# Latent attention of a four-layer kernel: its products from split operands instead of plain float32

## The chip, the cores and the metric

The program runs on one core of one Trainium2 chip. Its time is device microseconds of that core, from one launch; every number for a kernel is the median of several runs. TensorE (PE) multiplies and writes PSUM; VectorE (DVE), ScalarE (ACT) and GpSimd (POOL) work beside it; SyncE (SP) issues most of the DMAs.

## The reference

The reference is a stack of four layers on 512 latent tokens (and, in the first layer, 256 context tokens) of width 1024. The change touches the first layer's mixer, a multi-head latent attention with 8 heads. Cut to what matters:

```python
h_all = concat([h_ctx, h_lat])                       # T = 256 + 512 tokens, width 1024
cq = rms_norm(h_all @ w_dq, g_q)                     # rank 384
q = (cq @ w_uq).reshape(T, 8, 128 + 64)              # per head: 128 plain, 64 rotary
ckv = h_all @ w_dkv
c_kv = rms_norm(ckv[..., :256], g_kv)                # rank 256
kv = (c_kv @ w_ukv).reshape(T, 8, 128 + 128)         # per head: keys and values
k_rope = ckv[..., 256:]                              # 64 rotary columns, shared by the heads
# the rotary parts of the latent tokens are rotated
s = (q_nope @ k_nope.T + q_rope @ k_rope.T) * 192 ** -0.5
o = softmax(s) @ v       # latent tokens see all 768 keys, context tokens the 256 of the context
y = o @ w_o
```

All numbers are float32. The output is the last layer's latent tokens.

## The kernel before, in words

Activations are held transposed (width on the 128 partitions, the T = 768 tokens along the free dimension), in an area of SBUF called `arena`, which is why a trace names most tiles of the attention `arena`. A stage is a row of `STAGES`: its name, its iterations, its weight groups and its PSUM units per iteration. Weight groups come through a ring of two slots, `wring`, loaded by SP; a slot's next load waits until the group after it has started on PE (`w_used`). PSUM is used as two accumulators `acc[0]` and `acc[1]` (two banks each), taken in turn by consecutive units: `claim` waits until a unit's accumulator is free, `finished` until its products are done, `emptied` until an engine has copied it out. Two more such pairs, `sc[0]` and `sc[1]`, hold the scores.

In most stages (those in `SPLIT`) the operands are split. ACT copies a float32 weight into `w_hi`, which is rounded to float32r (`high_weights`, L1710), DVE subtracts to get `w_lo` (`split_weights`, L2399), activations are split likewise, and `split_product` makes each product from three matmuls: high by high, high by low, low by high. The stage `mla_pair`, which is changed, isn't among them: before, it works in plain float32, for which the trace shows two PE instructions a product.

`mla_pair` runs four times, with two heads in each iteration. An iteration has two parts.

**The projections.** Group 0 (`w_uq`, 3 blocks of 384 columns) gives unit 0 and 1 (plain queries of the two heads) and unit 2 (rotary queries of both); group 1 (`w_ukv`, 2 blocks of 512) gives units 3 and 4 (keys) and 5 to 7 (values, 2 token tiles each). DVE copies each unit out (L2323, L2326). Then two small matmuls (units 8 and 9, L960) rotate the rotary queries, and DVE puts them together (L2328 to L2337). PE waits for that (`qrope_ready`) before the first score.

**The loop over 12 score tiles** (6 per head: two of 256 keys, four of 768). For tile n: `turn(n)` transposes the probabilities on PE (L979), `scores(n + 2)` makes the scores of the tile after the next (L968, L970), `weigh(n)` multiplies by the values (L988). DVE finds the maximum (L2348) and its negative (L2350), copies out the result of tile n - 2 (L2341), takes the reciprocal of the sum (L2354), and does `in_attention(n)`, work for a later stage that has nothing to do with the attention (L2238, L2240, L2268, L2270). ACT makes the exponentials and their sum (L1696), copies the transposed probabilities of tile n - 1 out of PSUM (`turned`, L1688), and scales tile n (L1701). `weigh(n)` waits for `turned(n)`, which stands on ACT behind the exponentials of tile n + 1.

After the fourth iteration ACT loads a table, takes a small activation, loads the old table again (L1569, L1749), and splits the first group of `mla_out`, the output projection, together with DVE; then the attention's output is split block by block (L1717, L2376), and PE starts on `mla_out`.

Of the kernel before, what the change touches and what calls it, by code (L numbers as in the profile page):

```python
# [34 lines left out]
for _name, _n in [  # L35
# [16 lines left out]
    ("mla_in", 1, 2, 6), ("mla_rope", 1, 0, 2), ("mla_pair", 4, 2, 34), ("mla_out", 1, 4, 8),  # L52
# [10 lines left out]
SPLIT = ("mla_out", "mlp0", "gla_head", "gla_out", "mlp1", "gdn_gate", "gdn_pair", "gdn_out", "ffn0_up", "ffn0_down", "ret_head", "ret_out",  # L63
         "ffn1_up", "ffn1_down")
# [84 lines left out]
def first_and_second_block(nc, A, out):  # L149
    ctx = ExitStack()  # L150
    with ctx:
# [24 lines left out]
        eps = sb("eps", [P, 2])  # L176
        sq = sb("sq", [P, 2, T])
# [19 lines left out]
        with ExitStack() as plain:  # L197
            first("hT_", [P, DB, T])
            first("before_x_hi", [P, 2 * DB * T])
            x_hi_seq = first("x_hi_seq", [P, DB, SEQ], F32R)  # L200
        attn_lo = overlay("attn_lo", DB * T + ATTN_AT, [P, MLA_H, T])
# [50 lines left out]
        cq = carve(3, T)  # L252
        ckv = carve(2, T)
# [141 lines left out]
        lat_ready, krope_ready = sem("lat_ready"), sem("krope_ready")  # L395
        qrope_ready, s_ready = sem("qrope_ready"), sem("s_ready")
# [74 lines left out]
        def hole_parts(k):  # L471

            return [(0, SEQ, x_hole(k), x_lo[:, k, CTX:T])]

# [279 lines left out]
        def _(pe):  # L754
# [177 lines left out]
            pe.wait_ge(lat_ready, 5)  # L932
            pe.wait_ge(krope_ready, 2)
            S = "mla_pair"
            with pe.Fori(0, MLA_H // 2) as it:
                wq = group(S, it, 0, 3, 384)
                pe.wait_ge(uq_in, it * 48 + 48)
                for j, m in ((0, 0), (1, NOPE)):
                    claim(pe, S, it, j)
                    linear(unit(S, j), wq, m, lambda k: cq[:, k, :], T, 3).then_inc(acc_ready, 1)  # L940
                claim(pe, S, it, 2)
                linear(unit(S, 2), wq, 2 * NOPE, lambda k: cq[:, k, :], T, 3).then_inc(acc_ready, 1)
                wkv = group(S, it, 1, 2, 512)
                for j, m in ((3, 0), (4, 256)):
                    claim(pe, S, it, j)
                    linear(unit(S, j), wkv, m, lambda k: ckv[:, k, :], T, 2).then_inc(acc_ready, 1)
                wv = wkv.rearrange("p k (h s n) -> p k h s n", h=2, s=2)
                for j in range(3):
                    claim(pe, S, it, 5 + j)
                    for i in range(2):  # L950
                        t = 2 * j + i
                        for k in range(2):
                            last = mm(unit(S, 5 + j)[:, i, 0:256], ckv[:, k, t * P:(t + 1) * P],
                                      wv[:, k, :, 1, :], k == 0, k == 1)
                    last.then_inc(acc_ready, 1)

                emptied(pe, S, it, 2)
                for j in range(2):
                    claim(pe, S, it, 8 + j)
                    pe.matmul(unit(S, 8 + j)[:, 0, 0:256], rot2, qraw[:, CTX + 256 * j:CTX + 256 * (j + 1)],  # L960
                              start=True, stop=True).then_inc(acc_ready, 1)
                pe.wait_ge(qrope_ready, it * 1 + 1)

                def scores(n):
                    e, t = n // QT, n % QT
                    spans = [(0, 0, CTX)] if t < 2 else [(h, h * HALF, HALF) for h in range(2)]
                    for h, k0, w in spans:
                        pe.matmul(sc[:, n % 2, h, 0:w], qn[:, e, t * P:(t + 1) * P], kn[:, e, k0:k0 + w],  # L968
                                  start=True, stop=False)
                        last = pe.matmul(sc[:, n % 2, h, 0:w], qr[:, t * P:(t + 1) * P], krope[:, e, k0:k0 + w],  # L970
                                         start=False, stop=True)
                    last.then_inc(s_ready, 1)

                def turn(n):
                    nk = 2 if n % QT < 2 else KT
                    pe.wait_ge(p_ready, it * 12 + n + 1)
                    claim(pe, S, it, 10 + 2 * n)
                    for k in range(nk):
                        last = pe.transpose(flat(unit(S, 10 + 2 * n))[:, k * P:(k + 1) * P],  # L979
                                            prob[:, n % 2, k * P:(k + 1) * P], ident)  # L980
                    last.then_inc(acc_ready, 1)

                def weigh(n):
                    e, nk = n // QT, 2 if n % QT < 2 else KT
                    claim(pe, S, it, 11 + 2 * n)
                    emptied(pe, S, it, 10 + 2 * n)
                    for k in range(nk):
                        last = pe.matmul(unit(S, 11 + 2 * n)[:, 0, 0:P], vtok[:, k, e * P:(e + 1) * P],  # L988
# [2090 lines left out]
```

## Time and profile before

| | |
|---|---|
| median of 3 runs | 3701.36 us (3692.43 to 3707.0) |
| the profiled execution: its own time | 3693.87 us |
| the profiled execution: its span | 3692.2 us |
| granted TensorE clock, mean of the span | 0.976 of full speed |
| PE busy | 3456.4 us, 94% of the span |
| DVE busy | 1945.8 us, 53% |
| ACT busy | 1227.7 us, 33% |
| share of PE in the chain that ended last | 86% |
| the four iterations of `mla_pair` | start at 152.34, 230.49, 306.7 and 382.0 us; their first scores at 179.99, 255.82, 331.91 and 407.19 us; the last one ends at about 457 us |

An instruction's line number is that of the kernel before. A PE matmul's duration includes its pipeline; how fast matmuls follow one another is read from their starts.

### The profile page before, as it was taken

The numbers are of one execution on the slowest core, as the hardware profiler recorded it, in microseconds if no ns is written. First come the engines' busy times: TensorE is split into PE (matmuls) and PEld (weight loads), VectorE is DVE, ScalarE is ACT, GpSimd is POOL, SyncE is SP. The second block draws the span as 40 slices with busy tenths as digits, with TensorE's granted clock in tenths as the row PEclk, the third lists the DMA queues.
The fourth block names the chain that finished last, engine by engine and source line by source line (L and its number), as shares of the span: only waits on it lengthen the run. The fifth ranks groups of instructions, "written<-read, shape, count | busy, mean of one in ns | idle before, by whom it ended". The sixth has DMA issues, their size and how long they took to land.

```text
span 3692.2 us, 45549 instructions
## 1 busy us (share of the span) xinstructions
PE 3456.4 (94%) x17286; PEld 2863.0 (78%) x17286; DVE 1945.8 (53%) x2756; ACT 1227.7 (33%) x1580; POOL 230.0 (6%) x388
## 2 busy tenths in 40 slices
PE   7999899999997998899989999889998999899998
PEld 3566689999995887677768888768877777678876
DVE  4555446344445554644457766577735433455434
ACT  3033335123124333533344444333323222333332
POOL 0111001000000000111100000111100000000000
PEclk9999999999998999999999999999999999999999
DMA  6222113333231111344421111145533222222222
GB/s 211 80 61 61 45 46 115 96 119 106 92 108 37 41 40 57 114 159 156 159 92 47 34 45 46 46 154 179 178 101 100 68 68 68 66 83 91 91 86 85
DMA packets 294727, 335.34 MB, mean 91 GB/s; under 512 B 16466, under 2 KB 264146, under 8 KB 294482
## 3 DMA queue, kind: packets, MB, share of 16 engines
q1 hardware_dynamic: 261552, 232.93, 20.1%
q0 software_dynamic: 29440, 96.49, 8.3%
q10 hardware_dynamic: 3617, 4.26, 0.4%
q8 instruction: 85, 1.39, 0.2%
q14 instruction: 33, 0.26, 0.0%
HBM read 331.55 MB, written 2.10 MB: 90 GB/s over the span
## 4 chain that ended last, share of the span: by engine, by line
PE 86%; DVE 6%; DMA 3%; ACT 3%; issue 2%; ACTq 0%; DVEq 0%; POOL 0%; SPq 0%; POOLq 0%
PE acc L764 65%; PE sc L764 5%; PE sc L1354 2%; DMA wring<-in_mlp_w 1%; PE acc L988 1%; PE sc L904 1%; PE sc L968 1%; PE acc L1354 1%; PE acc L1533 1%; PE sc L970 1%; DVE w_lo L2399 1%; DVE arena L2152 0%; DVE d_col L2348 0%; PE acc L979 0%; DVE xT L2847 0%
## 5 line engine op out<-in xcount | busy, mean ns | idle before, releaser
L764 PE MATMUL acc<-x_lo,w_hi 128*128 128x512 f32 (+1 forms) x2208 | 834.8, 378 | 23.5 <-DVE g_out_lo L2376 8.3
L2399 DVE TENSOR_TENSOR w_lo<-wring,w_hi 128x1024 fp32r<-128x1024 f32 (+2 forms) x430 | 477.9, 1151 | 572.8 <-ACT w_hi L1710 572.0
L1710 ACT ACTIVATE w_hi<-wring 128x1024 fp32r<-128x1024 f32 (+2 forms) x432 | 409.9, 995 | 1016.5 <-DMA wring<-in_mlp_w 481.1
L764 PEld LDWEIGHTS acc<-x_lo,w_hi 128*128 128x128 f32 x2208 | 420.4, 190 | 91.9 <-DVE w_lo L2399 15.4
L764 PE MATMUL acc<-hid_hi,w_hi 128*128 128x512 f32 (+1 forms) x1120 | 413.6, 369 | 16.9 <-DVE w_lo L2399 8.9
L764 PE MATMUL acc<-hid_hi,w_lo 128*128 128x512 f32 (+1 forms) x1120 | 408.8, 365 | 0.0
L764 PE MATMUL acc<-x_hi_holes,w_hi 128*128 128x512 f32 x768 | 306.1, 399 | 17.0 <-DVE x_lo L2405 13.9
L764 PE MATMUL acc<-x_hi_holes,w_lo 128*128 128x512 f32 x768 | 304.4, 396 | 0.0
L764 PE MATMUL acc<-hid_lo,w_hi 128*128 128x384 f32 (+1 forms) x768 | 270.9, 353 | 0.0
L764 PEld LDWEIGHTS acc<-hid_hi,w_hi 128*128 128x128 f32 x1120 | 211.1, 188 | 45.3 <-DVE arena L2435 10.8
L764 PE MATMUL acc<-x_hi_seq,w_hi 128*128 128x512 f32 x576 | 228.6, 397 | 16.2 <-DVE x_lo L2408 13.7
L764 PEld LDWEIGHTS acc<-hid_hi,w_lo 128*128 128x128 f32 x1120 | 210.8, 188 | 24.4
L764 PE MATMUL acc<-x_hi_seq,w_lo 128*128 128x512 f32 x576 | 225.7, 392 | 0.0
L764 PE MATMUL acc<-x_hi,w_hi 128*128 128x384 f32 (+1 forms) x608 | 208.8, 343 | 11.2 <-DVE x_lo L2408 6.2
L764 PE MATMUL acc<-x_hi,w_lo 128*128 128x384 f32 (+1 forms) x608 | 207.4, 341 | 0.0
L764 PE MATMUL acc<-wide_lo,w_hi 128*128 128x512 f32 x480 | 188.5, 393 | 0.0
L764 PEld LDWEIGHTS acc<-x_hi_holes,w_hi 128*128 128x128 f32 x768 | 145.6, 190 | 52.5 <-issue 17.3
L764 PEld LDWEIGHTS acc<-x_hi_holes,w_lo 128*128 128x128 f32 x768 | 145.5, 190 | 33.5
L2229 DVE SCALAR_TENSOR_TENSOR tab<-rows_or_mod,cs,tab 128x512 f32<-128x512 f32 x204 | 148.0, 748 | 32.4 <-DMA rows_or_mod<-in_ada_w 29.0
L764 PEld LDWEIGHTS acc<-hid_lo,w_hi 128*128 128x128 f32 x768 | 144.3, 188 | 9.4
L748 POOL DMA_DIRECT2D rows_or_mod<-in_ada_w x176 | 94.9, 539 | 894.1 <-DVE tab L2229 391.6
L764 PEld LDWEIGHTS acc<-x_hi_seq,w_hi 128*128 128x128 f32 x576 | 109.2, 190 | 42.2 <-issue 19.9
(426 smaller groups left out, 6029.3 us busy)
## 6 DMA issues: line engine op xcount, KB each, us to landing
wring<-in_mlp_w SPq DMA_DIRECT2D x64, 1024.0 KB, 5.5
rows_or_mod<-in_ada_w POOLq DMA_DIRECT2D x208, 256.0 KB, 3.2
wring<-in_ffn_up SPq DMA_DIRECT2D x44, 1024.0 KB, 5.1
wring<-in_ret_w_in SPq DMA_DIRECT2D x24, 1024.0 KB, 5.2
rstd<-in_ada_w POOLq DMA_DIRECT2D x88, 256.0 KB, 3.4
wring<-in_ffn_down SPq DMA_DIRECT2D x32, 704.0 KB, 4.7
wring<-in_gdn_w_in SPq DMA_DIRECT2D x16, 1024.0 KB, 5.9
tab<-in_ada_w POOLq DMA_DIRECT2D x40, 256.0 KB, 3.4
```

The source lines that it names most:

```text
L748: pool.dma_start(mod_w[s], w[:, k, bass.ds(it * (per * MOD_N) + i * MOD_N, MOD_N)]).then_inc(mod_loaded[s], 16)
L764: ins = pe.matmul(o, lhsT, rhs, start=start, stop=stop)
L904: last = pe.matmul(mod_psum[:, bass.ds(it * (MOD_PIECES[phase] // DB * per * nv) + c, 1)], mod_acc[:, i % 2, v, m * P:(m + 1) * P], ones[: ...
L968: pe.matmul(sc[:, n % 2, h, 0:w], qn[:, e, t * P:(t + 1) * P], kn[:, e, k0:k0 + w], start=True, stop=False)
L970: last = pe.matmul(sc[:, n % 2, h, 0:w], qr[:, t * P:(t + 1) * P], krope[:, e, k0:k0 + w], start=False, stop=True)
L988: last = pe.matmul(unit(S, 11 + 2 * n)[:, 0, 0:P], vtok[:, k, e * P:(e + 1) * P], probT[:, n % 2, k * P:(k + 1) * P], start=k == 0, stop=k ...
L1354: last = pe.matmul(o[:, e, t], left[:, e, t], right[:, e, t], start=True, stop=True)
L1533: last = pe.matmul(unit(S, 8 + j)[:, i, t * P:SEQ], r_v[:, t, m // CTX, m % CTX:m % CTX + P], r_s[:, t, 0:SEQ - t * P], start=t == 0, stop ...
L1710: f(w_hi[s][:, c], wring[s][:, c], ACT.Copy).then_inc(w_high, 1)
L2229: ins = stt(a, mod_w[s], cs[:, k, v:v + 1], a, MUL, ADD)
L2399: tt(w_lo[s][:, c], wring[s][:, c], w_hi[s][:, c].bitcast(F32), SUB).then_inc(w_split, 1)
```

## The change: split operands in `mla_pair`

- `mla_pair` joins `SPLIT`. All products of its projections and of its scores are three float32r matmuls in place of one float32 product. The rotation, the transposes and `weigh` stay float32.
- Before the loop the normed inputs `cq` and `ckv` (now one tile `lat`) and the rotary keys `krope` are split by ACT (high) and DVE (low). PE's wait for all five blocks becomes a wait for each block.
- The queries, keys and rotary queries aren't copied out once by DVE, but split: ACT copies the high part out of PSUM (`high`), DVE subtracts for the low part (`low`) and frees the accumulator.
- The rotary queries come first (unit 0), then the plain ones (units 1 and 2). The rotation is one matmul of 512 columns into the score bank `sc[0, 0]`, between units 1 and 2, so there are 32 units for 34.
- The values are copied out by ACT, not DVE. The last of the three units of values comes behind `scores(0)` and `scores(1)`.
- The weights of group 0 of the next iteration are split in tiles 9 to 11 of the loop, half by half; those of group 1 between the query units. In the last iteration, which ACT and DVE now run outside of their hardware loops, the first group of `mla_out` is split there in place of after the loop.

The diff, cut to its core:

```diff
-    ("mla_pair", 4, 2, 34)
+    ("mla_pair", 4, 2, 32)
-SPLIT = ("mla_out", "mlp0", ...
+SPLIT = ("mla_pair", "mla_out", "mlp0", ...
+HALF_COLS["mla_pair", 0], HALF_COLS["mla_pair", 1] = 3 * 384 // 2, 512
...
# TensorE
-            pe.wait_ge(lat_ready, 5)
-            pe.wait_ge(krope_ready, 2)
+            pe.wait_ge(krope_ready, 4)
...
+                def queries(j, m):
                     claim(pe, S, it, j)
+                    for k in range(3):
+                        pe.wait_ge(lat_split, k + 1)
+                        last = split_product(unit(S, j), w, m, k, lat_parts(k), k == 0, k == 2)
+                    last.then_inc(acc_ready, 1)
+                w = split_group(S, it, 0, 3, 384)
+                second_half(S, it, 0)
+                queries(0, 2 * NOPE)
+                queries(1, 0)
+                emptied(pe, S, it, 0)
+                pe.matmul(sc[:, 0, 0, :], rot2, qraw[:, CTX:T], start=True, stop=True).then_inc(q_rot, 1)
+                queries(2, NOPE)
+                w = split_group(S, it, 1, 2, 512)
+                second_half(S, it, 1)
                 for j, m in ((3, 0), (4, 256)):
                     claim(pe, S, it, j)
+                    for k in range(2):
+                        pe.wait_ge(lat_split, 4 + k)
+                        last = split_product(unit(S, j), w, m, k, lat_parts(3 + k), k == 0, k == 1)
+                    last.then_inc(acc_ready, 1)
...
+                values(0)
+                values(1)
                 pe.wait_ge(qrope_ready, it * 1 + 1)
+                emptied(pe, S, it, 3)
+                emptied(pe, S, it, 4)
...  scores(n), in each of its spans
+                        for i, (q, k) in enumerate((
+                                (qn_hi[:, e, t], kn_hi[:, e, keys]), (qn_hi[:, e, t], kn_lo[:, e, keys]), (qn_lo[:, e, t], kn_hi[:, e, keys]),
+                                (qr_hi[:, t], krope_hi[e][:, keys]), (qr_hi[:, t], krope_lo[:, e, keys]), (qr_lo[:, t], krope_hi[e][:, keys]))):
+                            last = pe.matmul(sc[:, n % 2, h, 0:width], q, k, start=i == 0, stop=i == 5)
...
                 scores(0)
                 scores(1)
+                values(2)
# ScalarE, before the loop
             squares("cq", ...)
+            act.wait_ge(uq_in, 48)
+            high_weights("mla_pair", 0, 0)
             deviation("cq", T, Q_RANK)
             squares("ckv", ...)
-            act.wait_ge(lat_ready, 3)
+            act.wait_ge(krope_ready, 2)
+            for e in range(2):
+                f(krope_hi[e][:, :], krope[:, e, :], ACT.Copy).then_inc(krope_high, 1)
+            high_lat(range(3))
             deviation("ckv", T, KV_RANK)
+            high_lat(range(3, 5))
# ScalarE, an iteration
+                def high(j, hi):
+                    finished(act, S, it, j)
+                    f(halves(hi), unit(S, j)[:, :, 0:HALF], ACT.Copy).then_inc(qk_high, 1)
+                def values(j):
+                    finished(act, S, it, 5 + j)
+                    free(f(vtok[:, 2 * j:2 * j + 2, :], unit(S, 5 + j)[:, :, 0:256], ACT.Copy), S, 5 + j)
+                high(1, qn_hi[:, 0])
+                high_weights(S, it, 1)
+                high(2, qn_hi[:, 1])
+                act.wait_ge(qr_turned, it * 1 + 1)
+                f(qr_hi[:, :], qr, ACT.Copy).then_inc(qk_high, 1)
+                high(3, kn_hi[:, 0])
+                high(4, kn_hi[:, 1])
+                values(0)
+                values(1)
...  tile n
+                    if n == 0:
+                        values(2)
+                    if n in (9, 10):
+                        high_weights(*(("mla_out", 0, 0) if final else (S, it + 1, 0)), (n - 9,))
# VectorE, an iteration
+                def low(j, high, lo, hi):
+                    finished(dve, S, it, j)
+                    dve.wait_ge(qk_high, it * 5 + high)
+                    free(tt(halves(lo), unit(S, j)[:, :, 0:HALF], halves(hi).bitcast(F32), SUB), S, j)
+                finished(dve, S, it, 0)
+                free(cp(halves(qraw), unit(S, 0)[:, :, 0:HALF]), S, 0)
...
+                low(1, 1, qn_lo[:, 0], qn_hi[:, 0])
+                split_weights(S, it, 1)
+                dve.wait_ge(q_rot, it * 1 + 1)
+                st.did(tt(ktmp, sc[:, 0, 0, :], rsin, MUL))
                 st.settle()
+                tt(qr[:, CTX:T], qr[:, CTX:T], ktmp, ADD).then_inc(qr_turned, 1)
+                low(2, 2, qn_lo[:, 1], qn_hi[:, 1])
+                dve.wait_ge(qk_high, it * 5 + 3)
+                tt(qr_lo[:, :], qr, qr_hi[:, :].bitcast(F32), SUB).then_inc(qrope_ready, 1)
+                low(3, 4, kn_lo[:, 0], kn_hi[:, 0])
+                low(4, 5, kn_lo[:, 1], kn_hi[:, 1])
...  tiles 10 and 11
+                        split_weights(*(("mla_out", 0, 0) if final else (S, it + 1, 0)), (n - DB - 2,))
```

## Rows read from the trace of the kernel before

**Rows 1.** The page: engines' busy time, and the chain that ended last by engine.

```profile
PE 3456.4 (94%) x17286; PEld 2863.0 (78%) x17286; DVE 1945.8 (53%) x2756; ACT 1227.7 (33%) x1580; POOL 230.0 (6%) x388
...
PE 86%; DVE 6%; DMA 3%; ACT 3%; issue 2%; ACTq 0%; DVEq 0%; POOL 0%; SPq 0%; POOLq 0%
```

**Rows 2.** Stretches: stretch, us, busy (count) of PE, PEld, DVE, ACT, POOL; clock.

```profile
230.50:255.80 25.30, 23.31 (x82) 15.00 (x81) 9.25 (x14) 0.00 (x0) 0.00 (x0) 1.00 0.16 44
...
255.80:306.70 50.90, 48.29 (x269) 36.83 (x270) 29.77 (x72) 25.72 (x48) 7.20 (x12) 0.97 0.20 62
331.90:382.00 50.10, 46.66 (x269) 35.90 (x270) 29.79 (x72) 25.73 (x48) 7.20 (x12) 1.00 0.20 63
```

**Rows 3.** Timeline, second iteration's projections: start us, us, engine, line.

```profile
231.54 0.37 SPq L586 DMA_DIRECT2D wring<-in_mla_w_ukv  x1
234.64 0.96 DVE L2323 COPY arena<-acc 128x768 f32<-128x768 f32 x1 [3.92 <-PE acc L764]
238.51 0.96 DVE L2323 COPY arena<-acc 128x768 f32<-128x768 f32 x1 [2.91 <-PE acc L764]
...
255.82 1.09 PE L968 MATMUL sc<-arena 128*128 128x256 f32 x2 [1.65 <-DVE arena L2337]
```

**Rows 4.** Timeline, split products in `mla_out` and, from 1409.87, `gla_head`.

```profile
463.95 0.52 PE L764 MATMUL acc<-attn_lo,w_hi 128*128 128x384 f32 x1
...
467.15 0.52 PE L764 MATMUL acc<-x_lo,w_lo 128*128 128x384 f32 x1
...
470.00 0.33 PE L764 MATMUL acc<-x_lo,w_lo 128*128 128x384 f32 x1
...
475.72 0.33 PE L764 MATMUL acc<-x_lo,w_lo 128*128 128x384 f32 x1
...
1409.87 0.28 PE L764 MATMUL acc<-w_hi,x_hi 128*128 128x256 f32 x1
...
1411.91 0.28 PE L764 MATMUL acc<-w_lo,x_hi 128*128 128x256 f32 x1
```

**Rows 5.** Lines by form, ACT and DVE, us 90 to 480: busy us, mean ns.

```profile
L1688 ACT ACTIVATE arena<-acc 128x768 f32<-128x768 f32 x32 | 25.7, 804 | 7.4 <-PE acc L979 7.4
L1717 ACT ACTIVATE x_lo<-arena 128x768 fp32r<-128x768 f32 x8 | 6.0, 828 | 0.0
...
L2376 DVE TENSOR_TENSOR attn_lo<-arena,x_lo 128x768 fp32r<-128x768 f32 x8 | 7.0, 951 | 0.0
L2399 DVE TENSOR_TENSOR w_lo<-wring,w_hi 128x1024 fp32r<-128x1024 f32 x4 | 4.7, 1222 | 2.8 <-ACT w_hi L1710 2.8
```

**Rows 6.** Timeline, score tiles of the first iteration.

```profile
183.33 0.68 PE L979 MATMUL acc<-base_tab,arena 128*128 128x128 f32 x2 [0.41 <-ACT arena L1701]
...
190.46 0.95 DVE L2348 TENSOR_REDUCE d_col<-sc 128x1 f32<-128x768 f32 x1
...
194.07 0.95 DVE L2348 TENSOR_REDUCE d_col<-sc 128x1 f32<-128x768 f32 x1
...
198.35 0.96 DVE L2348 TENSOR_REDUCE d_col<-sc 128x1 f32<-128x768 f32 x1 [0.57 <-PE sc L970]
...
201.27 1.60 PE L988 MATMUL acc<-arena 128*128 128x128 f32 x12
...
208.87 0.96 DVE L2348 TENSOR_REDUCE d_col<-sc 128x1 f32<-128x768 f32 x1 [1.02 <-PE sc L970]
...
213.01 0.95 DVE L2348 TENSOR_REDUCE d_col<-sc 128x1 f32<-128x768 f32 x1
```

**Rows 7.** Timeline, before the first iteration and after the last.

```profile
144.45 2.88 DVE L2316 SCALAR_TENSOR_TENSOR arena<-arena,cols,rstd 128x768 f32<-128x768 f32 x3 [3.98 <-ACT rstd L1590]
...
152.34 0.50 PEld L764 LDWEIGHTS acc<-arena,wring 128*128 128x128 f32 x2 [2.70 <-issue]
...
459.03 2.00 ACT L1710 ACTIVATE w_hi<-wring 128x1024 fp32r<-128x1024 f32 x2
...
463.46 0.29 PEld L764 LDWEIGHTS acc<-x_lo,w_hi 128*128 128x128 f32 x1 [6.28 <-DVE w_lo L2399]
```

More of the change, by code:

```diff
@@ L51 @@
     ("ada", 1, 4, 0),
-    ("mla_in", 1, 2, 6), ("mla_rope", 1, 0, 2), ("mla_pair", 4, 2, 34), ("mla_out", 1, 4, 8),
+    ("mla_in", 1, 2, 6), ("mla_rope", 1, 0, 2), ("mla_pair", 4, 2, 32), ("mla_out", 1, 4, 8),
     ("mlp0", 4, 8, 16),
@@ L200, in first_and_second_block @@
             x_hi_seq = first("x_hi_seq", [P, DB, SEQ], F32R)
+        lat_hi, qr_hi, qn_hi = (overlay(f"{n}_hi", at * T, shape) for n, at, shape in (
+            ("lat", 0, [P, 5, T]), ("qr", 5, [P, T]), ("qn", 6, [P, 2, T])))
+        lat_lo, krope_lo = (overlay(f"{n}_lo", DB * T + at * T, shape) for n, at, shape in (
+            ("lat", 0, [P, 5, T]), ("krope", 5, [P, 2, T])))
+        krope_hi = [overlay(f"krope_hi{e}", DB * T + at, [P, T]) for e, at in ((0, 7 * T), (1, FFB * T + 4096 + 3072))]
+        qn_lo, qr_lo, kn_lo = (overlay(f"{n}_lo", DB * T + SEQ + at * T, shape) for n, at, shape in (
+            ("qn", 8, [P, 2, T]), ("qr", 10, [P, T]), ("kn", 12, [P, 2, T])))
         attn_lo = overlay("attn_lo", DB * T + ATTN_AT, [P, MLA_H, T])
@@ L251, in first_and_second_block @@
         at[0] = 0
-        cq = carve(3, T)
-        ckv = carve(2, T)
+        lat = carve(5, T)
+        cq, ckv = lat[:, 0:3], lat[:, 3:5]
         krope = carve(2, T)
@@ L931, in _ @@
             first_chunk(3)
-            pe.wait_ge(lat_ready, 5)
-            pe.wait_ge(krope_ready, 2)
[L934 to L988, printed above, removed]
-                                         probT[:, n % 2, k * P:(k + 1) * P], start=k == 0, stop=k == nk - 1)
-                    last.then_inc(acc_ready, 1)
-                scores(0)
-                scores(1)
-                for n in range(2 * QT):
-                    turn(n)
-                    if n == 9:
-                        first_sum(loop_piece(it, DB - 1) + 1, 0, lambda c: mod_psum[:, bass.ds(it * 8 + (MOD_AT + 32 + 8 * FIRST_CHUNKS + c), 1)])
-                    if n + 2 < 2 * QT:
-                        scores(n + 2)
-                    weigh(n)
-                pe.wait_ge(mod_used[(FIRST_LOOP - 1) % FIRST_SLOTS], loop_piece(it, FIRST_LOOP - 1) + 1)
-                for m in range(2):
-                    last = pe.matmul(mod_psum[:, bass.ds(it * 2 + (COND_AT + m), 1)], cond_acc[:, m * P:(m + 1) * P], ones[:, 0:1],
-                                     start=True, stop=True)
-                last.then_inc(first_summed, 1)
@@ L2312, in _ @@
             last.then_inc(krope_ready, 1)
-            for name, x, nb, g in (("cq", cq, 3, "mla_g_q"), ("ckv", ckv, 2, "mla_g_kv")):
+            S = "mla_pair"
+            split_weights(S, 0, 0)
+            for name, blocks, g in (("cq", range(3), "mla_g_q"), ("ckv", range(3, 5), "mla_g_kv")):
                 deviation_of(name)
-                for b in range(nb):
-                    stt(x[:, b, :], x[:, b, :], col(g, b), rstd[:, :], MUL, MUL).then_inc(lat_ready, 1)
-            S = "mla_pair"
+                for b in blocks:
+                    stt(lat[:, b, :], lat[:, b, :], col(g, b - blocks[0]), rstd[:, :], MUL, MUL).then_inc(lat_ready, 1)
+                if name == "cq":
+                    for e in range(2):
+                        dve.wait_ge(krope_high, e + 1)
+                        tt(krope_lo[:, e, :], krope[:, e, :], krope_hi[e][:, :].bitcast(F32), SUB).then_inc(krope_ready, 1)
+                for b in blocks:
+                    dve.wait_ge(lat_high, b + 1)
+                    tt(lat_lo[:, b, :], lat[:, b, :], lat_hi[:, b, :].bitcast(F32), SUB).then_inc(lat_split, 1)
```

126 lines of the change are left out of this document (91 added, 35 removed).

## The prediction, made before the changed kernel ran

> **What bounds the kernel now.** I read the page first: PE is busy 94% of the span and is 86% of the chain that ended last [rows 1]. That is an average; the change lies in 152 to 463 us, so I read that stretch alone. The stretches [rows 2] show two regimes. In the projections PE is busy 23.3 of 25.3 us and ACT does nothing at all. In a loop of score tiles PE is busy 46.7 of 50.1 us with DVE at 30 and ACT at 26. The clock is granted in full (2.4 GHz) in both but for 0.97 in one loop. So both parts are bound by PE, the loop with little in hand. Fewer PE cycles shorten the stage, up to where the chain over DVE and ACT takes over.
>
> **The rate of a product.** In plain float32 a unit of queries, 3 blocks in two halves of 384 columns, is 6 products or 12 instructions. DVE's copies of two such units start 3.87 us apart [rows 3]: 0.3225 us an instruction, 0.645 a product. Split products of the same width stand in `mla_out`: 33 follow one another from 470.00 to 475.72 [rows 4], 0.173 us each, 0.520 a product of three. For 256 columns, 17 in 2.04 us [rows 4] are 0.120 each, 0.360 a product; float32 by its columns is 0.430. So a product of 384 columns saves 0.125 us, one of 256 saves 0.07. That is 19% and 16%.
>
> The Trainium skill (TensorE: Matmul & The Clock Gate, Back-to-back issue gap) gives N / 2.4 + 2.5 ns for a warm gap, about 162 ns for 384 columns; this trace has 173 ns. By the page's figure an estimate would add some 40 x 4 x 3 x 0.011 = 5 us to the saving; the measurement decides.
>
> **Projections, without waits.** The queries have 18 products, the keys 8 (both of 384), the values 12 (of 256). After: 18 x 0.520 + 8 x 0.520 + 12 x 0.360 = 9.4 + 4.2 + 4.3 us. The rotation has the same 512 float32 columns as before, 0.86 us. One third of the values (1.45) moves behind the first scores. That leaves 17.3 us for PE up to the first score.
>
> **Projections, with waits.** Before, from 230.49 to the first score at 255.82, they took 25.3 us, where PE's own work was 22.8 (26 products of 0.645, 12 of 0.430, the rotation): the rest is the rotation at the end, where PE waits for DVE [rows 3]. After, the rotation stands between two query units and that stall goes. What is late next is the release of the accumulators. A unit of queries or keys is copied by ACT (0.80 for 768 from PSUM), then subtracted by DVE (0.95, row of 768 from SBUF) [rows 5], one behind the other, before its accumulator is free. I follow it from the first query product, 0:
> - Unit 0 to 3.1, unit 1 to 6.3, rotation to 7.1, unit 2 to 10.2. The load of group 1 is issued 1.05 us in [rows 3] and has five more before ACT asks for it.
> - ACT: `high` of unit 1 6.5 to 7.3, both weight halves (512 columns; 0.5 each, scaled from 1024 in 1.0 [rows 7]) to 8.4. DVE: `low` 7.4 to 8.4, weight halves (0.6 each, scaled from 1.22 [rows 5]) to 9.6, two rotation steps to 11.0, `low` of unit 2 to 12.3, `qr_lo` to 13.2.
> - Unit 3 10.2 to 12.3. Unit 4 needs the accumulator freed at 12.3: 12.5 to 14.5. Values 0 to 16.0. Values 1 need `low` of unit 4: ACT to 15.6, DVE to 16.6, so 16.7 to 18.2.
>
> So 18.2, to which I add 0.8 for waits on registers and hand-overs, which these sums leave out: 19.0. The gain is 6.2 us an iteration, 24.8 in four. Bounds: PE alone (17.3) gives 7.9 each, 31.6; if each of the four hand-overs costs one us more (23), 2.2 each, 9.
>
> **The loop.** A head has four tiles of 768 keys (4 products of 384) and two of 256 (2 products). PE saves 4 x 0.125 = 0.50 and 2 x 0.07 = 0.14 a tile, 4.3 us for both heads. A full tile costs PE 4.5 us before and 4.0 after. What may take over:
> - DVE's round from maximum to maximum, with one piece of `in_attention`, is 194.07 - 190.46 = 3.61 us when nothing else holds it; the next, 4.28, is held by PE [rows 6]. 3.61 fits in 4.0. With two cond pieces (tiles 8 and 9) it is 213.01 - 208.87 = 4.14 [rows 6], which doesn't.
> - `weigh(n)` starts 201.27 - 198.35 = 2.92 us after the maximum of tile n + 1 begins [rows 6]. Full tiles hide it behind 4.0 us; where a short tile's scores stand between (0.7 + 0.7 + 1.3), PE waits some 0.3.
> - ACT gets the weight halves behind tiles 9 and 10 (0.6 each; 1.0 in the last iteration), DVE behind 10 and 11. ACT has about one us in hand there, since DVE's round of 4.14 precedes; they cost nothing. If that cover is gone, they cost up to 1.6 an iteration.
>
> Following the tiles as above, I find gains of 0.3 at the first transposition, 1.7 at tile 5, 2.3 at tile 9, and 3.0 at the end of the loop. The first gap, from the first score at 179.99 to the first transposition at 183.33 [rows 6], takes the 1.45 us of the last values and hides them; uncovered they would cost 5.8 us in all. Four loops: 12 us, between 0 (all lost to DVE and ACT) and 17.
>
> **Before the first iteration.** ACT and DVE get the splits of `krope`, `lat` and group 0. DVE ends its three multiplications of `cq` at 147.33, from the start and length in [rows 7]. Two `krope_lo` and one `lat_lo` of about 0.9 follow (the pitch of L2376, 7.0 us for 8 [rows 5]), and PE starts at about 150.1 where it started at 152.34 [rows 7], since it no longer waits for `ckv`. ACT's `deviation` of `ckv` is 1.5 us later, but unit 3 is the first that needs it, 8 us behind. Slow clock at the start costs the same time as before. Gain 2.4, bounds 0 and 4.
>
> **Behind the last.** ACT no longer spends 2.00 us on the weights at 459.03 [rows 7], but splits the first block at once: 459.03 + 0.83 + 0.95 is 460.8 for PE, where it was 463.46. Gain 2.7, bounds 1 and 3.
>
> **The sum.** 24.8 + 12 + 2.4 + 2.7 = 42 us. The profiled execution took 3693.87 us (span 3692.2, 1.7 around it) and would take 3652. It lies 7.5 below the median of the runs shown, 3701.36, from which the sum gives 3659. I take 3656. Elsewhere nothing changes: the pieces of `in_attention` keep their order, so GpSimd's DMA queue does too, and SP's loads wait on the same first product of a group as before.
>
> **Rivals.**
> - *A wait for the one removed* (0.2). The two-step release (ACT, then DVE, 1.75 us and two hand-overs) sets the pace of units 2 to 5, since a keys unit costs PE only 2.1 us. For: only two accumulators, and the order on DVE puts the rotation's steps ahead of `low` of unit 2. Against: my own sum shows just 0.8 us of waits. With 3 us of waits more in each iteration, the gain is 30: 3668.
> - *PE stays the bound everywhere* (0.1): 31.6 + 17 + 4 + 3 = 56, 3643. For: DVE's 3.61. Against: the rounds of 4.14.
> - *The softmax chain sets the whole loop* (0.06), and the release the projections: gain under 18, 3686.
> - *Slower, by the clock* (0.03). At 463.95 to 467.15 ten split products of 384 columns took 0.32 us each, at 1.2 GHz, behind 6.3 us in which PE was idle [rows 4, 7]. Split products give PE more short waits. Each us of full-speed PE work done at the low level costs one us more, so the gain is gone once 42 of the stage's some 235 us of PE work fall there; with 60, about one iteration's work, the time is 3699 + 18 = 3717. Against: after waits of 1.65 us PE lost only some 0.8 us in one loop (0.97) and nothing in the other (1.00) [rows 2], and the new waits are shorter. The Trainium skill (TensorE: Matmul & The Clock Gate, HAM oscillation) has this as a rule: gaps of PE bring the low clock back. By that rule, the trace agrees only in so far as the long idle time of [rows 7] was followed by it.
>
> **How the numbers follow.** My forecast, a gain of 34 to 50, gets 0.61. The likeliest is 3656. Gains of 18 to 62 us against a kernel between 3694 and 3701 hold 8 in 10: 3635 to 3680. A measurement of this kernel tells 0.5%, 18.5 us, from no change. Faster: forecast, first two rivals, 0.91. Within 0.5%: 0.06. Slower: 0.03.
>
> **What would show it.** Right: `mla_pair` iterations of about 66 us for 76; the first score 19 us after the first query product; split instructions 0.173 us apart in the scores; transpositions 4.0 to 4.2 us apart in full tiles; PE on `mla_out` within 2 us of the table load. Wrong: PE idle over 3 us in the projections, behind `low` or `high`; a granted clock under 0.9 in the stage; the first iteration's start not before 152.

## The result, and the profile after

The changed kernel takes 3650.86 us (median of 4 runs, 3650.12 to 3656.44), beside 3701.01 us (3692.43 to 3707.0, 4 runs) for the kernel before: a ratio of 0.9869, 95% interval 0.9857 to 0.9881. The forecast was 3656, with a range of 3635 to 3680. The profiled execution has an own time of 3650.92 us and a span of 3649.2, 43.0 less than before.

The page of the kernel after, which answers to [rows 1]:

```profile
PE 3428.0 (94%) x17590; PEld 2896.1 (79%) x17590; DVE 1957.4 (54%) x2767; ACT 1264.6 (35%) x1635; POOL 229.9 (6%) x388
...
PE 85%; DVE 7%; ACT 3%; issue 2%; DMA 2%; ACTq 0%; DVEq 0%; POOL 0%; SPq 0%; POOLq 0%
```

PE has 304 instructions more and is busy 28 us less: float32 products take two instructions each and split ones three, but shorter ones. The averages say no more than that. The stretches do, in the columns of [rows 2]: the projections of the first and second iteration, then the loops of the first and third.

```profile
148.65:168.38 19.73, 19.27 (x105) 18.41 (x105) 14.27 (x18) 8.42 (x12) 0.00 (x0) 0.91 0.20 58
216.43:234.61 18.18, 17.71 (x106) 16.84 (x106) 9.27 (x13) 5.62 (x8) 0.00 (x0) 1.00 0.22 61
168.38:216.43 48.05, 44.42 (x323) 41.95 (x321) 30.97 (x74) 28.08 (x52) 7.20 (x12) 1.00 0.22 67
300.84:348.89 48.05, 44.40 (x322) 41.92 (x321) 30.96 (x74) 28.10 (x52) 7.19 (x12) 1.00 0.21 66
```

The bounds of each stretch are instructions of PE: the first query product, the first score, the next iteration's first query product. The same places in the trace of before make this table (us):

| | before | after | gain |
|---|---|---|---|
| first query product | 152.34 | 148.65 | 3.69 |
| projections, 4 iterations | 27.65, 25.33, 25.33, 25.34 | 19.73, 18.18, 18.18, 18.34 | 7.92 + 7.15 + 7.15 + 7.00 = 29.2 |
| loop, 3 iterations | 50.50, 50.76, 49.94 | 48.05, 48.05, 48.05 | 2.45 + 2.71 + 1.89 = 7.05 |
| last first score to PE on `mla_out` | 56.30 | 51.70 | 4.60 |
| PE's start on `mla_out` | 463.49 | 418.93 | 44.6 |
| from there to the end of the span | 3228.7 | 3230.3 | -1.6 |

So the whole gain stands in the stretch that the change touches, two thirds of it in the projections, and the code behind it, which is the same, gave 1.6 back.

**Projections.** The timeline of ACT and DVE in the second iteration of the kernel after, for [rows 3]:

```profile
219.86 0.96 DVE L2415 COPY arena<-acc 128x768 f32<-128x768 f32 x1 [3.20 <-PE acc L779]
...
222.98 0.81 ACT L1733 ACTIVATE qn_hi<-acc 128x768 fp32r<-128x768 f32 x1 [8.42 <-PE acc L779]
...
226.96 0.81 ACT L1733 ACTIVATE qn_hi<-acc 128x768 fp32r<-128x768 f32 x1 [2.13 <-PE acc L779]
...
227.81 0.96 DVE L2412 TENSOR_TENSOR qn_lo<-acc,qn_hi 128x768 fp32r<-128x768 f32 x1 [0.50 <-ACT qn_hi L1733]
228.68 0.95 DVE L2427 TENSOR_TENSOR qr_lo<-arena,qr_hi 128x768 fp32r<-128x768 f32 x1
229.89 0.96 DVE L2412 TENSOR_TENSOR kn_lo<-acc,kn_hi 128x768 fp32r<-128x768 f32 x1 [0.26 <-ACT kn_hi L1733]
232.06 0.96 DVE L2412 TENSOR_TENSOR kn_lo<-acc,kn_hi 128x768 fp32r<-128x768 f32 x1 [1.21 <-ACT kn_hi L1733]
```

Unit 0 is copied 3.4 us after the first product at 216.43, unit 1 at 6.55, unit 2 at 10.5: units of 3.1 us and 0.86 for the rotation between units 1 and 2, as added up. DVE now ends `qr_lo` at 229.6, five us before the first score at 234.61, where DVE's last step of the rotation had held PE for 1.65 us in [rows 3]. In place of that wait stands one short one, in the last `low` before values 1. The waits of PE from 216 to 283 us (us in total, times, longest):

```profile
PE acc L1034 <- ACT arena L1757: 3.2, 6, 1.0
PE acc L779 <- DVE kn_lo L2412: 0.5, 1, 0.5
PE acc L1025 <- ACT arena L1770: 0.4, 2, 0.2
```

The first row belongs to the loop: `weigh` waits for ACT's copy of the transposed probabilities. The second is all that the two-step release costs PE. The rate of the products, in PE's timeline, is that of [rows 4]: values from 167.07 to 168.26 (10 in 1.19 us, 0.119 each), scores from 339.75 to 340.62 (5 in 0.87, 0.174 each).

```profile
166.85 0.38 PE L779 MATMUL acc<-w_hi,lat_hi 128*128 128x256 f32 x1 [0.46 <-DVE kn_lo L2412]
167.07 0.28 PE L779 MATMUL acc<-w_hi,lat_lo 128*128 128x256 f32 x1
...
168.26 0.28 PE L779 MATMUL acc<-w_lo,lat_hi 128*128 128x256 f32 x1
168.38 0.28 PE L1017 MATMUL sc<-kn_hi,qn_hi 128*128 128x256 f32 x1
...
339.75 0.34 PE L1017 MATMUL sc<-kn_hi,qn_hi 128*128 128x384 f32 x1
...
340.62 0.34 PE L1017 MATMUL sc<-krope_hi,qr_lo 128*128 128x384 f32 x1
```

**Loop.** The timeline of full tiles in the third iteration after, for [rows 6]:

```profile
310.14 0.87 PE L1025 MATMUL acc<-base_tab,arena 128*128 128x128 f32 x6 [0.18 <-ACT arena L1770]
...
310.37 0.95 DVE L2441 TENSOR_REDUCE d_col<-sc 128x1 f32<-128x768 f32 x1
...
313.97 0.95 DVE L2441 TENSOR_REDUCE d_col<-sc 128x1 f32<-128x768 f32 x1
...
314.73 0.82 PE L1025 MATMUL acc<-base_tab,arena 128*128 128x128 f32 x6
...
317.50 1.50 PE L1034 MATMUL acc<-arena 128*128 128x128 f32 x12
...
317.70 0.96 DVE L2441 TENSOR_REDUCE d_col<-sc 128x1 f32<-128x768 f32 x1
...
318.84 0.82 PE L1025 MATMUL acc<-base_tab,arena 128*128 128x128 f32 x6
```

The maxima are 3.60 and 3.73 us apart. The transpositions of tiles 3 and 4 (314.73 and 318.84) are 4.11 apart, and at 318.84 PE has no wait in front of it. The same transpositions in the third iteration before, and then those of tiles 5 and 9 before and after:

```profile
341.70 0.82 PE L979 MATMUL acc<-base_tab,arena 128*128 128x128 f32 x6
...
346.27 0.82 PE L979 MATMUL acc<-base_tab,arena 128*128 128x128 f32 x6
...
350.85 0.82 PE L979 MATMUL acc<-base_tab,arena 128*128 128x128 f32 x6
...
354.08 0.82 PE L979 MATMUL acc<-base_tab,arena 128*128 128x128 f32 x6
...
368.74 0.82 PE L979 MATMUL acc<-base_tab,arena 128*128 128x128 f32 x6
```

```profile
322.07 0.82 PE L1025 MATMUL acc<-base_tab,arena 128*128 128x128 f32 x6
...
336.25 0.82 PE L1025 MATMUL acc<-base_tab,arena 128*128 128x128 f32 x6
```

From tile 3 to tile 4 it was 4.58 us and is 4.11, nearly all that PE saves in a full tile. From tile 2 to tile 3 it was 4.57 and is still 4.59. So the saving comes through in some tiles and not in others.

**Entry and exit.** The timelines around the first query product and around `mla_out`, for [rows 7]:

```profile
148.65 0.53 PE L779 MATMUL acc<-lat_hi,w_hi 128*128 128x384 f32 x1 [0.35 <-DVE lat_lo L2404]
...
415.65 1.28 ACT L1598 ACT_TABLE_LOAD   x1
416.95 3.04 ACT L1788 ACTIVATE x_lo<-arena 128x768 fp32r<-128x768 f32 x4
...
418.93 0.66 PE L779 MATMUL acc<-x_lo,w_hi 128*128 128x384 f32 x1 [3.74 <-DVE attn_lo L2476]
```

Of the 3.69 us at the entry 1.46 are older than the change: the square sums of `cq` on PE, which no edit touches, start at 137.04 before and at 135.58 after. What is left, 2.23 us, is the entry's own. The twelve traces below agree: the square sums start anywhere from 135.1 to 138.7, and the first query product comes 12.8 to 13.3 us behind them, where before it came 15.3 behind. At the exit ACT goes from the table load straight to the first block, and PE starts 2.0 us after the load ends.

### The profile page after: what moved, and what is told of

It is laid out like the page before. It is cut to its first block, busy times and chain, and to the rows that moved or that the text cites. A ratio compares the mean times of both kernels' runs of the same rounds, so it can differ in the third digit from the quotient of the medians.

```text
span 3649.2 us, 46202 instructions
## 1 busy us (share of the span) xinstructions
PE 3428.0 (94%) x17590; PEld 2896.1 (79%) x17590; DVE 1957.4 (54%) x2767; ACT 1264.6 (35%) x1635; POOL 229.9 (6%) x388
## 4 chain that ended last, share of the span: by engine, by line
PE 85%; DVE 7%; ACT 3%; issue 2%; DMA 2%; ACTq 0%; DVEq 0%; POOL 0%; SPq 0%; POOLq 0%
PE acc L779 65%; PE sc L779 5%; PE sc L1383 2%; PE sc L919 1%; PE acc L1383 1%; PE acc L1562 1%; PE acc L1034 1%; DVE d_col L2441 1%; DMA wring<-in_mlp_w 1%; PE sc L1017 1%; DVE w_lo L2385 1%; DVE arena L2222 0%; PE acc L1355 0%; DVE xT L2937 0%; DVE xT L2226 0%
## 5 line engine op out<-in xcount | busy, mean ns | idle before, releaser
L2385 DVE TENSOR_TENSOR w_lo<-wring,w_hi 128x1024 fp32r<-128x1024 f32 (+3 forms) x446 | 489.0, 1136 | 567.2 <-ACT w_hi L1707 566.4
L1707 ACT ACTIVATE w_hi<-wring 128x1024 fp32r<-128x1024 f32 (+3 forms) x448 | 419.9, 983 | 1016.4 <-DMA wring<-in_mlp_w 479.4
L779 PEld LDWEIGHTS acc<-hid_hi,w_hi 128*128 128x128 f32 x1120 | 211.3, 189 | 40.3 <-DVE w_lo L2385 10.2
```

The costliest lines, as they stand in the source:

```text
L779: ins = pe.matmul(o, lhsT, rhs, start=start, stop=stop)
L1707: f(w_hi[s][:, c], wring[s][:, c], ACT.Copy).then_inc(w_high, 1)
L2385: tt(w_lo[s][:, c], wring[s][:, c], w_hi[s][:, c].bitcast(F32), SUB).then_inc(w_split, 1)
```

## The experiments

Each kernel is the changed one with the edit shown, timed beside the kernel before on the same chip (medians of that one: 3696.08, 3703.2, 3700.47 and 3696.45 in the four groups). Totals of this kernel scatter more than most edits are worth; "Why" below shows it. Hence each experiment is read first from the lengths of projections and loop in its trace, in the bounds of the table above. Where kernels share the code of a stretch and its clock is 1.00, most of these lengths repeat within 0.05 us, over iterations and kernels (the last iteration's projections are some 0.15 longer in all of them).

The question of the first four: PE lost 4.5 us of work on scores in a loop (four products of 384 columns in each of eight tiles, two of 256 in each of four), and the loop became shorter by 1.9 to 2.7. PE's busy time in it fell by less, from 46.7 to 44.4, since the last values now stand in it; `e6_values_before` below shows that they cost nothing there. What sets the loop now?

**Fewer products, more products.** `e1_four` leaves the two low-by-high products out of each score, `e2_eight` adds the two low-by-low ones.

```diff
-  (qn_hi, kn_hi), (qn_hi, kn_lo), (qn_lo, kn_hi), (qr_hi, krope_hi), (qr_hi, krope_lo), (qr_lo, krope_hi)
+  (qn_hi, kn_hi), (qn_hi, kn_lo), (qr_hi, krope_hi), (qr_hi, krope_lo)                  # e1_four
+  ... (qn_lo, kn_hi), (qn_lo, kn_lo), ... (qr_lo, krope_hi), (qr_lo, krope_lo)           # e2_eight
```

> Each score span is made from four products for six: low query by high key is left out for both parts, so this kernel leaves out part of the computation. Theory A (mine, from the profile after): the loop of score tiles is no longer held by PE but by DVE's round of maximum, wait for the exponentials, reciprocal and in_attention (3.61 us a tile); then PE's 0.69 us less in a full tile and 0.24 in a short one (6.5 us a loop) comes through only where PE stands on the chain (scores 0, 8 and 11), 1.5 to 2.2 us a loop: 3643. Theory B (PE still the bound of full tiles, as the prediction had it for tiles 2 to 7): 6.5 us a loop, 26 in all: 3625.

> Low by low is added to each score span, eight split matmuls for six, so PE's scores cost 2.77 us in a full tile, a little over the 2.58 of plain float32. Theory A: a full tile then costs PE 4.8 us and the loop is held by PE again, as before: 51 to 52 us for 48, 3663 to 3667; the rate of the scores is then worth less than half of the 6.5 us a loop by which PE's work grows. Theory B: 6.5 us a loop, 3677.

Measured: `e1_four` 3653.4 us (0.9879, 0.9862 to 0.9895), loops of 46.35 to 46.38, 1.68 shorter, for 6.5 us of PE work taken away. `e2_eight` 3669.01 us (0.992, 0.9903 to 0.9936), loops of 51.41 to 51.43, 3.37 longer, for 6.5 us added. PE alone would give 6.5 both ways, a chain without PE nothing. A quarter comes through on one side and half on the other.

**Less DVE work.** `e3_small` makes each piece of `in_attention` work on 32 of its 512 columns (16 of 256 in the cond pieces).

```diff
-  a = first_acc[:, i % 2, v, :]
+  a, w = first_acc[:, i % 2, v, 0:n], first_w[s][:, 0:n]      # n = 32
```

> in_attention works on 32 of 512 (and 16 of 256) columns, so that its result is incomplete; its loads, waits and counts stay. Theory A: without the 1.42 us of a piece DVE's round is some 2.4 us, PE holds the loop (41.9 us of its own work), which falls from 48.0 to some 45.5: 3641, and the transpositions of full tiles stand 4.0 us apart. Theory B: no change, since PE holds the loop already: 3651.

Measured: 3649.02 us (0.9865, 0.9846 to 0.9884), loops of 46.40 to 46.41: 1.65 shorter, for 9.1 us of DVE work less (30.96 to 21.86). The windows of one loop, `e1_four` first, then `e3_small`:

```profile
235.33:281.68 46.35, 38.42 (x282) 35.23 (x281) 30.75 (x74) 28.05 (x52) 7.18 (x12) 1.00 0.22 68
```

```profile
234.99:281.39 46.40, 43.71 (x322) 41.96 (x321) 21.86 (x74) 27.84 (x52) 7.17 (x12) 1.00 0.21 68
```

In `e1_four` PE idles for 7.9 us of its loop and most of that is one kind of wait, for the copy of the transposed probabilities, which stood at 3.2 in the kernel after. In `e3_small` it is DVE that has the time, and waits for scores:

```profile
PE acc L1034 <- ACT arena L1757: 7.4, 8, 1.4
```

```profile
DVE d_col L2441 <- PE sc L1017: 10.6, 7, 2.8
```

**Order on DVE.** `e4_piece_first` puts the piece of `in_attention` ahead of the wait for the exponentials and the reciprocal, so that DVE works while ACT does.

```diff
-  dve.wait_ge(p_exp, it * 12 + n + 1)
-  dve.reciprocal(small[:, s, 3:4], small[:, s, 2:3]).then_inc(p_inv, 1)
   in_attention(it, n)
+  dve.wait_ge(p_exp, it * 12 + n + 1)
+  dve.reciprocal(small[:, s, 3:4], small[:, s, 2:3]).then_inc(p_inv, 1)
```

> DVE does its piece of in_attention while it waits for the exponentials, before the reciprocal, not behind it. Theory A: the 0.7 us that DVE waits in each round are filled, the round is some 3.1 us, and full tiles are held by PE: 1.5 to 2 us less a loop, 3643 to 3645. Rival: the reciprocal is late, ACT's scaling waits for it (tiles 8 and 9 with two pieces above all), and nothing is won or up to 1 us a loop lost: 3651 to 3655.

Measured: 3652.22 us (0.9879, 0.9863 to 0.9896), loops of 48.10 to 48.15: no change. The third transposition comes 9.72 us after the first score instead of 9.3, since the reciprocal is late; the full tiles then run at PE's 4.1 us and the start is made up. That left a third theory: PE (4.1 us a full tile) and the round over DVE and ACT (3.6, and 4.14 with two cond pieces) are so near to each other that either takes over at once when the other gets shorter.

**Both at once.** `e9_four_small` is `e1_four` and `e3_small` together.

> Both at once: four products in a score span and pieces of 32 columns; so two parts of the computation are left out. Alone, each made a loop 1.65 us shorter (46.4 for 48.05), against 6.5 us of PE work and 11 us of DVE work removed. Theory C (new: PE's work and DVE's round are nearly equal in full tiles, so that taking away one leaves the other): together they give clearly more than 3.3 us a loop, 43 us or less. Rival D (a third chain, maximum to exponentials to copied transposition to weigh, or ACT's own work, holds both): together 46.4 to 44.7, no more than the sum of the two.

Measured: 3635.25 us (0.9824, 0.9808 to 0.9841), loops of 42.82 to 42.83, 5.23 shorter. The two alone gave 1.68 and 1.65, 3.33 together; the other 1.9 us show only when both are gone. The window of a loop, two maxima of DVE, and two of the waits in this window:

```profile
231.61:274.43 42.82, 38.03 (x283) 35.40 (x281) 21.80 (x74) 27.80 (x52) 7.20 (x12) 1.00 0.23 73
```

```profile
302.92 0.96 DVE L2441 TENSOR_REDUCE d_col<-sc 128x1 f32<-128x768 f32 x1 [0.40 <-PE sc L1017]
...
306.45 0.96 DVE L2441 TENSOR_REDUCE d_col<-sc 128x1 f32<-128x768 f32 x1 [0.81 <-PE sc L1017]
```

```profile
PE acc L1034 <- ACT arena L1757: 4.2, 7, 1.0
ACT arena L1765 <- DVE d_col L2443: 9.1, 9, 2.1
```

The round is 3.53 us with no engine full: DVE waits for PE's scores, PE for ACT's copy, and ACT for DVE's maximum. What is left is a chain of latencies through all three. No run made ACT's own work shorter; in the kernel after it waits 15.3 us in a loop for DVE's maxima, so its busy time isn't the bound there.

**The rotation back to the end.** `e5_rot_late` puts the rotation, DVE's two steps on it and ACT's `qr_hi` behind the values, as before the change.

```diff
-                emptied(pe, S, it, 0)
-                pe.matmul(sc[:, 0, 0, :], rot2, qraw[:, CTX:T], start=True, stop=True).then_inc(q_rot, 1)
                 queries(2, NOPE)
...
                 values(1)
+                emptied(pe, S, it, 0)
+                pe.matmul(sc[:, 0, 0, :], rot2, qraw[:, CTX:T], start=True, stop=True).then_inc(q_rot, 1)
```

> The rotation goes back behind the values, and with it DVE's two steps and both halves of the split of the rotated queries. Theory A (the place of the rotation hides its chain): the first score waits for rotation 0.85, two DVE steps 1.4, ACT 0.85, DVE 0.95 and hand-overs, some 4.4 us an iteration more, 3668. Rival (the queries' and keys' releases set the end of the projections anyway): under 1.5 us an iteration, 3656.

Measured: 3674.11 us (0.9927, 0.9906 to 0.9947), span 3670.0, 20.8 more than the kernel after. Projections of 21.88, 3.70 longer, and loops of 49.17 to 49.39, 1.1 to 1.35 longer although their code is the same. PE's timeline in the third iteration, and the window of that loop:

```profile
314.54 0.39 PE L1017 MATMUL sc<-kn_hi,qn_hi 128*128 128x256 f32 x1 [3.37 <-DVE qr_lo L2429]
...
315.12 0.28 PE L1017 MATMUL sc<-krope_lo,qr_hi 128*128 128x256 f32 x1
...
316.60 0.41 PE L779 MATMUL acc<-w_lo,lat_hi 128*128 128x256 f32 x1
...
318.52 0.41 PE L779 MATMUL acc<-w_lo,lat_hi 128*128 128x256 f32 x1
```

```profile
314.54:363.71 49.17, 45.63 (x320) 43.56 (x321) 30.95 (x74) 27.38 (x51) 7.18 (x12) 0.97 0.21 64
```

PE idles for 3.37 us and restarts at 2.4 GHz (0.12 us a product); from 315.96 on the products stand 0.213 us apart (9 of values in 1.92), which is 1.2 GHz, up to 319.0, and the loop has a clock of 0.97. The same happens in the first two iterations, 0.6 and 1.0 us after the restart, for 3.2 us each. In the fourth iteration, behind the same wait (3.38), it doesn't: the loop was granted 1.00. So the place of the rotation is worth 3.70 us an iteration, nearly all of it the wait, and in three of four iterations up to 1.35 more by the clock. The Trainium skill (TensorE: Matmul & The Clock Gate, HAM oscillation) states that a long wait of PE brings the low clock back and that the work behind the wait starts slow. This trace agrees in part: a fall to the low clock followed three of four such waits, but each time PE first ran at 2.4 GHz for 0.6 to 1.4 us.

**The last values back before the scores.** `e6_values_before`:

```diff
                 values(1)
+                values(2)
                 pe.wait_ge(qrope_ready, it * 1 + 1)
...
                 scores(1)
-                values(2)
```

> The third unit of values comes before the first scores again. Theory A (the gap before the first transposition hides it): 1.45 us an iteration more, 3657. Rival (ACT's copy behind tile 0 costs the loop as much as the cover saves): 3651.

Measured: 3657.26 us (0.9882, 0.9861 to 0.9903); projections of 19.60, 1.42 longer, loops of 48.03, the same within 0.02. The gap behind the first scores hides the whole unit, 5.7 us in four iterations.

**The weights of `mla_out` back behind the loop.** `e7_out_after`:

```diff
-                    if n in (9, 10):
-                        high_weights(*(("mla_out", 0, 0) if final else (S, it + 1, 0)), (n - 9,))
+                    if n in (9, 10) and not final:
+                        high_weights(S, it + 1, 0, (n - 9,))
...
+            high_weights("mla_out", 0, 0)
             out_highs("mla_out", [attn[:, b, :] for b in range(MLA_H)])
```

> The first group of the output projection is split behind the loop again, by ACT and DVE. Theory A: PE starts on it 2.6 us later, 3653.5, the last loop unchanged or 0.2 shorter. Rival (the weight halves in tiles 9 to 11 held up the last loop): the last loop is over 1 us shorter, and the sum is 3652 or less.

Measured: 3654.03 us (0.9873, 0.985 to 0.9896). From the last first score to `mla_out` 54.18 us, where it was 51.70: 2.48 us, once, with the loops the same (48.04 to 48.06). In the total this can't be told. The first projections took 18.20 us in this trace, at a clock of 1.00, where the same code took 19.73 at 0.91 in the kernel after: what the start costs by the clock differs from run to run.

**Two units of values behind the scores.** `e8_values_later` puts `values(1)` there too, with its copy on ACT behind tile 0's scaling and that of `values(2)` in tile 1.

```diff
                 values(0)
-                values(1)
...
                 scores(1)
+                values(1)
                 values(2)
```

> The second unit of values also comes behind the first scores, so the first scores no longer wait behind the release of the last keys and those values (1.9 us); ACT copies them behind tile 0 and inside tile 1. If the loop is held by DVE's rounds, which begin with the first maximum, it comes 1.5 us earlier an iteration and about half is lost again since scores(2) come later: 2 to 4 us in all, 3647 to 3649. Rival: PE's 2.9 us of values between scores(1) and the first transposition delay scores(2) by as much as was won: 3651.

Measured: 3650.49 us (0.9857, 0.9835 to 0.9879); projections 1.57 shorter (16.61), loops 1.03 longer (49.08). The gap takes one unit for nothing; of a second one, two thirds of the time come back in the loop.

**Two cures for the tiles with two pieces.** `e10_early` does the first two pieces of `in_attention` in the projections, where DVE is idle, so that tile n does piece n + 2 and none has two cond pieces. `e11_sum_late` moves the 8 small products of `first_sum` on PE from tile 9 to tile 11.

```diff
+                in_attention(it, 0)                              # e10_early
+                in_attention(it, 1)
                 finished(dve, S, it, 0)
...
-                    if n == 9:                                   # e11_sum_late
+                    if n == 11:
                         first_sum(loop_piece
```

> The first two pieces of in_attention go before DVE's first copy of an iteration, where it waits for the rotary queries (3.4 us idle for 2.3 of work); each of tiles 0 to 9 then has one piece, so no round has two. If the rounds of 4.14 in tiles 8 and 9 hold the loop, it falls by some 1 us of the 1.65 that the removal of all pieces gave: 47.0 for 48.05, projections unchanged but for the first iteration (up to 2 us longer, since DVE comes late from the splits). Rival: the place is taken from PE's slower path (tiles 2 to 7), under 0.3 us.

> The 16 one-column matmuls of first_sum (1.68 us), which stand in tile 9 before the last scores, go behind the last transposition, where PE waits 1.0 us for ACT's copy. The last scores come up to 1.6 us earlier and 0.7 us is paid back at the end: 0.9 us a loop, 47.1 for 48.05. Rival (DVE's round of tile 10, with its weight half, holds the last maximum): under 0.3 us won, or a loss up to 0.7.

Measured: `e10_early` 3650.88 us (0.9866, 0.985 to 0.9883), loops of 47.45 to 47.47, 0.59 shorter, projections the same but for the first, 0.7 longer. `e11_sum_late` 3651.26 us (0.9871, 0.9854 to 0.9887), loops of 46.95 to 46.97, 1.09 shorter.

**All three.** `e12_all` is `e8_values_later`, `e10_early` and `e11_sum_late` together.

> The three edits that shortened an iteration together: first pieces before the projections' first copy (0.6 us), first_sum behind the last transposition (1.1), two units of values behind the first scores (1.6 less in the projections, 1.0 more in the loop). If they add up, an iteration takes 64.0 us for 66.23 (projections 16.6, loop 47.4), 9 us in all: 3642. If PE's later scores(2) become the bound once DVE's rounds are shorter, the values' edit turns to nothing and it is 64.5 to 65: 3645. The total scatters by some 5 us from run to run, so the iteration's length in the trace decides.

Measured: 3647.51 us (0.986, 0.9839 to 0.9881). Projections of 16.61, loops of 46.99 to 47.00: an iteration of 63.6 for 66.2. From the first query product to PE's start on `mla_out` it takes 259.57 us, the kernel after 270.28: 10.7 less. In an iteration that is 2.6 us, where the three alone add up to 0.59 + 1.09 + 0.54 = 2.2. A part of the 10.7 is the clock of the first projections, which was 1.00 here as in `e7_out_after`. The total fell by 3.3 us at the median and the intervals overlap, so in the total a gain over the changed kernel isn't shown.

## Why the prediction was right, step by step

By their places the terms add up to 43.1 us where 42 were forecast (44.6 less the 1.46 at the square sums). That they come so near is partly luck: the projections gave 4.4 us more than forecast and the loops 2.9 less, and the two errors cancel. One by one:

- **Rate of a product: right.** 0.174 and 0.119 us stand where 0.173 and 0.120 were taken from `mla_out` and `gla_head`.
- **Projections: right in the bare sum, too careful in the addition.** The sum followed gave 18.2; 18.18 was measured, in two iterations alike, and no unit on the way lies over 0.15 us from its place in the sum (unit 3 starts at 10.3 for 10.2, the values at 14.6 for 14.5). The 0.8 us for waits on registers and hand-overs were not needed, which is 3.2 us in four. The term was 24.8 and is 29.2. Of the other 1.2 us, 0.8 are from the first iteration: the slow clock at the start was to cost the same as before, and cost 2.3 us before (27.65 less 25.33) and 1.55 after (19.73 less 18.18). That part is luck; `e7_out_after` shows the same code start without it. The rest is rounding.
- **The wait in place of the one removed** (0.2) didn't come. PE waits once, for 0.5 us. `e5_rot_late` shows what the order avoided: 3.70 us an iteration.
- **The last values are hidden: right.** `e6_values_before`, 1.42 us against 1.45.
- **Loop: the mechanism right, the size too large.** The term was 3.0 an iteration and 12 in all; the three whole loops gave 2.45, 2.71 and 1.89, and the last some 2.1 (4.60 less the 2.48 of `e7_out_after`), 9.1 in all. The transpositions show where it falls short. Counted from the first score, they come earlier than in the third loop of before by 0.25 us at the first tile, 0.95 at tile 5, 1.42 at tile 9 and 1.89 at the end of the loop; 0.3, 1.7, 2.3 and 3.0 were forecast. The rows for the tiles [rows 6] were those of the first loop, which had a stretch at the low clock in it (0.97, 50.50 us long where the third, at 1.00, took 49.94). Against that loop the gains are 0.34, 1.50, 1.97 and 2.45. So about half of what is missing is that stretch of clock, and the rest, 0.55 us, arises along the whole loop, from tiles whose saving didn't come through. `e11_sum_late` and `e10_early` show two places where the loop still loses time, behind PE's small products in tile 9 and DVE's double pieces in tiles 8 and 9 (1.09 and 0.59); both stood in the kernel before too. PE's saving itself was added up a little too low: eight tiles of 0.50 and four of 0.14 are 4.6 us, not 4.3. What was priced too high is the share of it that comes through.
- **What sets the loop.** "Up to where the chain over DVE and ACT takes over" was right, nearer than I thought: neither PE alone (`e1_four`) nor DVE alone (`e3_small`) sets it, and both together give 1.9 us more than the sum of the two. For the two rivals of the loop this settles both: PE isn't the bound everywhere, since 4.5 us less work gave 1.9 where the clock was full on both sides; and the softmax chain doesn't set the whole, since that 1.9 did come, and 1.68 more in `e1_four`. (`e2_eight` alone wouldn't show it: with more work PE could become the bound of a loop that it didn't hold before.)
- **Entry: right,** 2.23 for 2.4 (the two starts given there, 150.1 and 152.34, are 2.2 apart). **Exit: right,** 2.48 for 2.7.
- **The estimate of 5 us beside the rate of a product** counts 40 products of 384 columns in an iteration. There are 26 in the projections and 32 in the loop, which makes it 7.7 us; the forecast doesn't use it.
- **Slower, by the clock** (0.03) didn't come: all loops and all projections but the first were granted 1.00, more than before. The mechanism exists, as `e5_rot_late` shows, at 1.1 to 1.35 us behind a wait of 3.37, in three iterations of four.

**Totals and places.** The medians lie 50 us apart, the two traces 43. Both are measurements of the same change. The time from PE's start on `mla_out` to the end of the span, the same code in every kernel here, was 3228.7 us before, 3230.3 after, and in the twelve experiments between 3225.2 (`e4_piece_first`) and 3240.0 (`e8_values_later`). A part of it can be seen in one stretch, most of `mlp1` and the products just ahead of it, here in the kernel after and then in `e8_values_later`:

```profile
1434.50:1823.50 389.00, 374.33 (x1646) 302.30 (x1645) 203.19 (x260) 143.45 (x193) 55.22 (x97) 0.99 0.46 151
```

```profile
1435.70:1830.40 394.70, 376.04 (x1646) 303.82 (x1646) 202.94 (x260) 143.44 (x193) 55.34 (x97) 0.99 0.46 149
```

The same instructions and the same clock take 5.7 us more, of which only 1.7 are PE's busy time; PE's waits for DVE's additions (L2526 in the kernel after) are 2.9 us in the one and 6.9 in the other. The DMA share is 0.46 there, for about 0.21 in the changed stage; that the transfers are what varies, and hold up DVE and so PE, is likely but not shown. So a total of this kernel tells some 5 us, and it takes the places in a trace to tell one. The forecast of 3656 was set between the sum against the profiled execution (3652) and the sum against the median (3659); how near it came to 3650.86 is partly that scatter.

## What to carry to other kernels

Follow a stage by hand over all its engines, unit by unit, from measured durations: here the bare sum was right within 0.1 us, and the allowance on top of it was the error. Where two engines' rounds are within some 15% of each other (4.1 and 3.6 to 4.14 us), price a saving on one well below its work (here 1.65 us of 9.1, 1.68 of 6.5, and 1.9 of 4.5 for the change itself: a fifth to two fifths) and look for the other's edit that releases the rest. Count a gain from a stretch at full clock, and judge small edits by the length of their own stage, not by the total.

## What the runs showed of the hardware

- Behind a wait of PE of 3.37 us (`e5_rot_late`) the clock fell to 1.2 GHz in three of four iterations, 0.6 to 1.4 us after PE's restart and for some 3.2 us, and in the fourth it didn't. Behind waits of 1.65 us before the change it fell in two of four. The loops of the kernel after, with waits of up to 1.0 us, were all granted 1.00.
- The stretches of one stage repeat within some 0.05 us over iterations and kernels at full clock, while 3,230 us of identical code with heavy transfers differ by up to 15 us.
- A split product of three float32r instructions takes 0.52 us at 384 columns where a float32 one takes 0.645, although it has three instructions for two.
